# A bias table kept once as eight rows, and copied to 128 rows per head from memory to memory behind the input projection

## What is computed

```python
z = x @ w_in + b_in                       # columns: mLSTM group and sparse-attention (NSA) group
h = mlstm_chunkwise(...)                  # 8 heads of 64
o_c, o_s, o_w = nsa_attend(...)           # compressed, selected and window branch, 8 heads of 64
x1 = layer_norm(ALPHA * x + mix @ w_out, ln1_w, ln1_b)
u = causal_dwconv(x1 @ w_up + b_up, ...)
y = layer_norm(ALPHA * x1 + (gelu(u[..., :D_FF]) * u[..., D_FF:]) @ w_down + b_down, ln2_w, ln2_b)

def t5_bucket(dist):                      # 32 log buckets of the distance
    n = jnp.maximum(dist, 0)
    ...
    return jnp.where(n < max_exact, n, large)

def head_bias(rel_bias, dist):            # added to every NSA logit
    b = rel_bias[t5_bucket(dist)].astype(jnp.float32)
    ...
```

## Time and profile before

| | |
|---|---|
| median of 3 runs | 1063.69 us |
| lowest and highest | 1063.34 and 1071.04 us |
| profiled execution | 1065.43 us |
| its span in the profile | 1063.7 us |
| TensorE busy | 921.4 us, 87% of the span |
| VectorE busy | 517.3 us, 49% |
| ScalarE busy | 374.3 us, 35% |
| GpSimd busy | 99.3 us, 9% |
| moved by transfers | 112.44 MB, mean 106 GB/s |

### The profile page before, as it was taken

The page is one execution under the profiler, slowest core; times in us unless marked ns, Lnnn a source line. Parts: engine busy times, 40 slices in busy tenths (PEclk is TensorE's granted clock), DMA queues, the critical chain, the costliest instruction groups (busy, mean ns, idle before and its releaser), DMA issues.

```text
span 1063.7 us, 19859 instructions
## 1 busy us (share of the span) xinstructions
PE 921.4 (87%) x7903; PEld 824.2 (77%) x7903; DVE 517.3 (49%) x1116; ACT 374.3 (35%) x742; POOL 99.3 (9%) x164
## 2 busy tenths in 40 slices
PE   5865898899988758698888976999999999999994
PEld 5764687677877647355557966999999999999992
DVE  3610224642233564666664237667676676422325
ACT  4220234463532010155563136343443434222215
POOL 1001121334344000200000000000000000000000
PEclk9976898999999555558899998999999999999997
DMA  8256677757735000220003211232222222222212
GB/s 284 79 114 142 192 234 263 239 191 222 214 108 200 1 6 1 94 118 1 1 1 124 80 40 40 80 99 80 86 95 79 99 81 77 90 80 87 87 32 85
DMA packets 53135, 112.44 MB, mean 106 GB/s; under 512 B 6945, under 2 KB 30274, under 8 KB 52594
## 3 DMA queue, kind: packets, MB, share of 16 engines
q1 hardware_dynamic: 44616, 89.06, 25.3%
q0 software_dynamic: 6528, 17.83, 5.3%
q10 hardware_dynamic: 1898, 4.27, 2.5%
HBM read 102.92 MB, written 12.38 MB: 108 GB/s over the span
## 4 chain that ended last, share of the span: by engine, by line
PE 76%; DVE 9%; DMA 5%; ACT 4%; issue 3%; SPq 2%; ACTq 0%; POOLq 0%; POOL 0%; DVEq 0%
PE q L1667 28%; PE q L1665 26%; DMA arena<-in_pool 5%; PE q L2112 2%; PE q L2130 2%; PE q L2140 2%; PE q L1729 1%; PE q L2000 1%; PE q L2173 1%; PE q L2174 1%; PE q L2054 1%; PE q L1717 1%; PE q L1783 1%; PE q L1963 1%; DVE xt L1529 1%
## 5 line engine op out<-in xcount | busy, mean ns | idle before, releaser
L468 DVE TENSOR_TENSOR wring_r<-wring,whi_r 128x1024 fp32r<-128x1024 f32 (+1 forms) x101 | 120.5, 1193 | 366.9 <-ACT whi_r L465 366.7
L465 ACT ACTIVATE whi_r<-wring 128x1024 fp32r<-128x1024 f32 (+1 forms) x101 | 104.2, 1033 | 325.0 <-PE q L1667 314.3
L1667 PE MATMUL q<-xt_r,whi_r 128*128 128x288 f32 x552 | 167.7, 304 | 0.0
L1665 PE MATMUL q<-xt_r,whi_r 128*128 128x256 f32 x552 | 158.2, 287 | 0.0
L1665 PE MATMUL q<-arena_r,whi_r 128*128 128x256 f32 x440 | 138.0, 314 | 19.7 <-DVE xt_r L468 11.6
L1667 PE MATMUL q<-arena_r,whi_r 128*128 128x288 f32 x440 | 134.3, 305 | 0.0
L1667 PE MATMUL q<-arena_r,wring_r 128*128 128x288 f32 x440 | 133.5, 303 | 0.0
L1665 PE MATMUL q<-arena_r,wring_r 128*128 128x256 f32 x440 | 126.5, 287 | 0.0
L1665 PE MATMUL q<-mixt_r,whi_r 128*128 128x256 f32 x400 | 113.0, 282 | 10.5 <-DVE xt_r L468 10.5
L1667 PE MATMUL q<-mixt_r,whi_r 128*128 128x288 f32 x400 | 119.2, 298 | 0.0
L1665 PEld LDWEIGHTS q<-xt_r,whi_r 128*128 128x128 f32 x552 | 107.7, 195 | 0.0
(11 more groups left out here) (406 smaller groups left out, 1584.4 us busy)
## 6 DMA issues: line engine op xcount, KB each, us to landing
wring<-in_w_up SPq DMA_DIRECT2D x42, 512.0 KB, 3.3
wring<-in_w_in SPq DMA_DIRECT2D x27, 512.0 KB, 5.2
arena<-in_pool SPq DMA_DIRECT2D x64, 192.0 KB, 3.8
arena<-in_pool POOLq DMA_DIRECT2D x64, 192.0 KB, 4.2
wring<-in_w_down SPq DMA_DIRECT2D x24, 448.0 KB, 3.2
arena<-in_pool POOLq DMA_DIRECT2D x64, 64.0 KB, 2.5
arena<-in_pool SPq DMA_DIRECT2D x64, 64.0 KB, 2.2
wring<-in_w_out SPq DMA_DIRECT2D x8, 512.0 KB, 6.1
```

The lines of the kernel that those rows point to most:

```text
L465: return eng.activation(out, src, ACT.Copy)
L468: return eng.tensor_tensor(out, src, hi.bitcast(F32), ALU.subtract)
L1665: pe.matmul(out[:, 0, 0:HALF], w, x[:, 0:HALF], start=(kk == 0 and n == 0), stop=(end and n == 2))
L1667: mm = pe.matmul(out[:, 1, 0:HALF + NS], w, x[:, HALF:NT], start=(kk == 0 and n == 0), stop=(end and n == 2))
```

## The change

A second array in the chip's memory, relone of 8 x 640, takes the table once: ScalarE's transfer at tile 4 goes there. The copy to 128 rows per head, relrow, is issued by SyncE behind its projection loop, from relone; it waits for the first transfer (rel_out at 16), and the shifted load waits for the second as well (rel_out at 32). No other instruction is changed. All lines behind the first edit stand one line lower than before, those behind the second three, and those behind the third two.

```diff
         relrow = nc.dram_tensor("relrow", (H, 128, NREL), F32, kind="Internal")
+        relone = nc.dram_tensor("relone", (H, NREL), F32, kind="Internal")
...
             sp.wait_ge(rel_out, 16)
+            sp.dma_start(relrow.ap(), relone.ap().unsqueeze(1).broadcast_to([H, 128, NREL])).then_inc(rel_out, 16)
+            sp.wait_ge(rel_out, 32)
             sp.wait_ge(nd_mx, GROUPS)
             shifted = bass.AP(tensor=relrow, offset=127, ap=[[NREL - 1, 128], [128 * NREL, H], [1, 512]])
             sp.dma_start(tb, shifted).then_inc(tb_in, 16)
...
                 if n == 4:
                     act.wait_ge(rel_sb, 1)
-                    act.dma_start(relrow.ap(), ohp[0:8, NREL:2 * NREL].unsqueeze(1).broadcast_to([8, 128, NREL])) \
-                        .then_inc(rel_out, 16)
+                    act.dma_start(relone.ap(), ohp[0:8, NREL:2 * NREL]).then_inc(rel_out, 16)
                     act.wait_ge(g_col, 1)
```

## The result

The changed kernel takes 1033.61 us (median of 4 runs, 1029.32 to 1037.76) against 1064.23 us before (4 runs): a ratio of 0.9698 with a 95% interval of 0.9642 to 0.9755. That is 30.6 us less. The profiled execution is the longest of its runs, 1037.76 us with a span of 1036.1, so the two profiled spans differ by 27.6 us only.

A forecast was written before the change was run, and what follows sets the result against it. Up to 112 us the kernel was taken to run at the pace of page loads, slowed by the table's copy. From 1063.7 us, 35.1 gained and 0 for the moved copy gave 1029, range 1023 to 1041.

The forecast's parts named there:

- The size: Between the first two score matmuls: without the large copy at tile 4, 51.36 us become 16.3, a gain of 35.1.
- The period: Time between the first two score matmuls, four page beats; forecast to fall from 51.36 us to 16 to 18.
- the lower bound of 24.8 us: Early page stream: only the TensorE's waits for pages go, its clock stays low; total 1039 us, chance 0.07 as a rival.
- the bounds of 24.8 and 38.5: Early page stream: gain in us from the waits alone, and from matmul rates in a wider window; totals 1039 and 1025.
- All follows the TensorE: Behind the early page stream: all later work stands behind the TensorE in its order, so the 35.1 us should reach the end.
- Part two: Behind SyncE's projection loop: the memory-to-memory copy, taken as 16 us, is hidden and adds 0.
- cover: Behind the projection loop: the copy may land 75 us after its issue before anyone waits.
- The seam rival: Behind the projection loop: the new copy catches the last value pages and costs up to 11 us; 1040 us, chance 0.06.
- the slow rival: Behind the projection loop: a very slow copy makes the states late, costing from 75 us on; 1084 at 130 us, chance 0.04.
- few engines: Old copy at tile 4: eight as outermost dimension confines it to at most eight engines, so pages crossing them land late.
- The sentence on the two ports: Old copy at tile 4: source partitions 0 to 7 lie on two ports of 27.2 GB/s, an estimated 48 us for 2.62 MB.

The follow-up runs named there:

- again: The changed kernel measured once more without any edit: 1033.21 us, ratio 0.9704 to the kernel before.
- half: The kernel before with 64 instead of 128 rows per head in its large copy, the shifted load taking both halves from them: 1045.44 us, ratio 0.9812.
- x8: The changed kernel with its large copy behind the projection loop made eight times, one after the other: 1075.17 us, ratio 1.0082 to the kernel before.
- spread8: The kernel before with the large copy's eight table rows on partitions 0, 4, ..., 28 instead of 0 to 7: 1037.39 us, ratio 0.9720.
- spread4: The kernel before with the large copy's eight table rows on partitions 0, 2, ..., 14 instead of 0 to 7: 1038.95 us, ratio 0.9767.
- x4: The changed kernel with its large copy behind the projection loop made four times, one after the other: 1031.06 us, ratio 0.9650 to the kernel before.
- noseam: The changed kernel without any large copy, the shifted load reading page data instead, so the bias is wrong: 1030.82 us, ratio 0.9665 to the kernel before.
- early8: The changed kernel with its memory-to-memory copy put back on ScalarE at tile 4, behind the small copy, eight still outermost: 1034.27 us, ratio 0.9701.

## Why the prediction was right

**The size.** The period is 16.48 us in the first profile and 15.82 in the second, a gain of 34.9 and 35.5 against the 35.1 forecast. The clock did come back with the waits: 1.00 where the lower bound of 24.8 us had it stay. The medians gained 30.6 and, in the second measurement (again), 33.6 us; both lie within the bounds of 24.8 and 38.5. The first two profiled spans differ by 27.6 us, 7.3 less than the 34.9 of the period. Of these, 2.5 were lost ahead of the first mark, where the second profile does not lose them, and 2.4 in the woven part behind the second mark, where the two profiles of the changed kernel differ by more than that. The last 2.3 lie behind the last score matmuls: from there to the end are 789.0 us before and 791.3 after, but also 791.1 in half, whose seam is that of the kernel before.

**All follows the TensorE.** Held: x8 aside, every kernel whose first period shrank became faster by about as much (half: 21.4 us of period, 21.3 of time; spread8: 31.5 and 29.2; spread4: 27.4 and 25.0).

**Part two costs nothing.** Held, with a copy of 16.1 us for the 16 that were taken, and a cover of 80.6 us for the 75 that were worked out. The seam rival (1040) fell with x4 and noseam. From the last score matmuls to the end noseam has 788.1 us and x4 790.2, against 791.3 and 791.1 in the changed kernel, so up to some 3 us are left that these profiles can't tell from chance. No wait of the TensorE, VectorE or ScalarE between the copy's issue and 480 us was for a transfer. The price of the slow rival was right too: eight copies, about 122 us, brought the kernel to 1075 us.

**The cause was half named.** The prediction said that the old copy makes the pages late, and this is shown: half of it gives back about half of the time, and cheaper forms of the same copy nearly all. But it leaned on few engines, and on the eight as outermost dimension, as the reason. early8 keeps the eight and the place, and costs 2 us; spread8 keeps the source's memory as well. The price was right all the same, because it was read from the periods and needed no reason for the slow pages. The rival that bytes in the ramp cost what they cost was not given in the prediction, and would have been wrong by 33 us. What the runs showed in place of that step is the source: eight neighbouring partitions, which made each row three times as dear (0.33 us against 0.106). The sentence on the two ports, which the prediction had only beside its sum, is the one that the runs bear out, with the open end named under spread4. Hence the move behind the projection loop was not needed for the gain: the small copy, which changes the source from the core's memory to the chip's, is what brought it.

**Open.** Why the woven part of one kernel spreads over 5.5 us from run to run isn't settled. The two profiles have mean clocks of 0.95 and 0.97 there, and 3.6 and 1.3 us of waits for pages of keys; whether one causes the other was not tried. And no version was found that beats the changed kernel beyond the intervals.

## What to carry to other kernels

A transfer that nobody waits for can still cost much (35 us here), if it takes the engines that a tight stream needs: look at what its queue held of the engines' time per row, not at its bytes, and at whether a slow stretch begins and ends with it. When a small table is spread out many times over, put it into memory first or lay its rows four partitions apart; where the cheap copy then stood mattered little here, as long as nobody waited for it (x8). To size such an edit, compare a mark that comes round in the slow stretch and behind it with equal work between, as the waits alone miss what the lower clock costs (24.8 us of 35).

## What was not expected of the hardware

2560-byte rows out of the core's memory took 0.33 us of an engine each when eight neighbouring partitions were the source, 0.148 with every second partition and 0.106 with every fourth, the last as much as from the chip's memory (0.107). While the dear ones were in flight, pages of 192 KB on other queues took 17.7 us to land instead of about 3; beside the copy from memory they took 7.3, and the TensorE waited 1.6 us in all. A copy of 2.62 MB from memory to memory took 16.1 us with eight rows outermost, up to the issue that waited for it, and at most 12.3 with 128.
